# Attention gate's projection as three rounded passes, its rests made by GpSimd

## The reference, cut to what matters

```python
for l in range(DEPTH):                      # 2 layers
    h = rmsnorm_2(x, norm_g[l])             # (256, 1024)
    proj = h @ w_in[l]                      # all projections of the layer
    q, k, v, ga, iq, ik, iw, xr, gr, ma, mb = jnp.split(proj, offsets, axis=-1)
    ...
    attn = dsa_attention(q, k, v, iq, ik, iw).reshape(B, S, ATTN_WIDTH_2)   # 8 heads x 128
    y_a = (attn * jax.nn.silu(ga)) @ w_out_attn[l]
    ...
    hr = rg_lru(xr, w_rg[l], b_rg[l], w_ig[l], b_ig[l], lru_lambda[l])      # a scan over tokens
    y_b = (hr * jax.nn.silu(gr)) @ w_out_rnn[l]
    merged = jax.nn.sigmoid(ma) * y_a + jax.nn.sigmoid(mb) * y_b
    x = x + merged @ w_o[l]
```

## Time and profile before

| what | before |
|---|---|
| median of 3 runs | 1917.48 us |
| lowest, highest | 1916.91, 1917.63 us |
| the profiled execution, its own time | 1915.96 us |
| its span, first to last instruction | 1914.2 us |
| PE (TensorE) busy | 1854.3 us, 97% of the span |
| DVE (VectorE) busy | 833.7 us, 44% |
| ACT (ScalarE) busy | 670.1 us, 35% |
| POOL (GpSimd) busy | 268.8 us, 14% |
| mean granted TensorE clock | 0.992 of full speed |

### The profile page before, as it was taken

The page is one execution under the profiler, slowest core; times in us unless marked ns, Lnnn a source line. Parts: engine busy times, 40 slices in busy tenths (PEclk is TensorE's granted clock), DMA queues, the critical chain, the costliest instruction groups (busy, mean ns, idle before and its releaser), DMA issues.

```text
span 1914.2 us, 28319 instructions
## 1 busy us (share of the span) xinstructions
PE 1854.3 (97%) x11306; PEld 1257.3 (66%) x11306; DVE 833.7 (44%) x1889; ACT 670.1 (35%) x1287; POOL 268.8 (14%) x239
## 2 busy tenths in 40 slices
PE   9999999999999999999999999999999999999998
PEld 8774444444447874444434446888989978888997
DVE  5763121211215762112211114566665655667655
ACT  5632111111114631111111113457664544575544
POOL 1400000000000400000000003972000057800000
PEclk9999999999999999999999999999999999999999
DMA  8569999999996469999999996452524845433353
GB/s 297 225 237 416 428 427 427 429 428 428 429 424 226 189 274 399 412 427 427 428 428 429 429 427 241 143 207 89 173 92 154 280 171 176 174 136 104 118 170 134
DMA packets 121430, 557.58 MB, mean 291 GB/s; under 512 B 5008, under 2 KB 49584, under 8 KB 96240
## 3 DMA queue, kind: packets, MB, share of 16 engines
q1 hardware_dynamic: 119696, 551.51, 72.5%
q10 hardware_dynamic: 1440, 4.36, 0.6%
q0 software_dynamic: 192, 0.30, 0.1%
HBM read 555.11 MB, written 1.05 MB: 291 GB/s over the span
## 4 chain that ended last, share of the span: by engine, by line
PE 58%; DVE 4%; DMA 3%; ACT 3%; issue 2%; POOL 0%; SPq 0%; POOLq 0%; DVEq 0%; ACTq 0%
PE bank L2322 7%; PE bank L2353 5%; PE bank L2471 3%; PE bank L2473 3%; PE bank L2472 3%; DMA ring<-w_up_dram 3%; PE bank L2450 3%; PE bank L2451 3%; PE bank L2452 3%; PE bank L2324 3%; PE bank L2557 3%; PE bank L2045 2%; PE bank L2420 2%; PE bank L2054 2%; PE bank L2487 1%
## 5 line engine op out<-in xcount | busy, mean ns | idle before, releaser
L2322 PE MATMUL bank<-ring,work 128*64 128x512 f32 x544 | 242.6, 601 | 13.4 <-issue 13.4
L1663 DVE TENSOR_TENSOR work<-work,bank 64x512 f32<-64x512 f32 x64 | 43.9, 685 | 440.0 <-ACT work L1004 440.0
L2324 PE MATMUL bank<-ring,work 128*64 128x512 f32 x512 | 232.3, 609 | 0.0
L776 POOL TENSOR_TENSOR stat<-stat,power 128x1 f32<-128x1 f32 (+1 forms) x18 | 10.8, 600 | 1496.5 <-DVE stat L1235 959.9
L816 POOL TENSOR_TENSOR w_lo<-ring,w_hi 128x512 fp32r<-128x512 f32 (+1 forms) x160 | 208.1, 1317 | 53.6 <-ACT w_hi L1054 50.8
L1004 ACT ACTIVATE work<-bank 64x512 f32<-64x512 f32 x64 | 37.8, 591 | 466.5 <-PE bank L2324 466.5
L1054 ACT CAST w_hi<-ring 128x512 fp32r<-128x512 f32 (+1 forms) x208 | 123.3, 606 | 120.8 <-PE bank L2473 81.5
L2353 PE MATMUL bank<-ring,work 128*64 128x512 f32 x480 | 155.8, 595 | 1.8 <-ACT work L1009 0.4
L2322 PEld LDWEIGHTS bank<-ring,work 128*64 128x64 f32 x544 | 73.1, 138 | 125.5 <-issue 123.6
L1883 DVE TENSOR_TENSOR w_lo<-ring,w_hi 128x512 fp32r<-128x512 f32 (+1 forms) x176 | 116.3, 678 | 79.0 <-ACT w_hi L1159 78.7
L1679 DVE SCALAR_TENSOR_TENSOR act_hi<-bank,stat,act_hi 128x512 fp32r<-128x512 f32 x64 | 48.1, 751 | 211.1 <-ACT act_hi L1014 211.1
(11 more groups left out here) (354 smaller groups left out, 4489.4 us busy)
## 6 DMA issues: line engine op xcount, KB each, us to landing
ring<-w_in_dram SPq DMA_DIRECT2D x34, 2048.0 KB, 9.0
ring<-w_gate_dram SPq DMA_DIRECT2D x34, 2048.0 KB, 21.1
ring<-w_up_dram SPq DMA_DIRECT2D x32, 2048.0 KB, 26.6
ring<-w_down_dram SPq DMA_DIRECT2D x30, 2048.0 KB, 26.0
ring_tail<-w_down_dram SPq DMA_DIRECT2D x18, 2048.0 KB, 24.1
work<-w_gate_dram SPq DMA_DIRECT2D x16, 2048.0 KB, 21.8
work<-w_up_dram SPq DMA_DIRECT2D x16, 2048.0 KB, 26.2
ring_tail<-w_up_dram SPq DMA_DIRECT2D x16, 2048.0 KB, 27.2
```

The costliest lines, as they stand in the source:

```text
L2322: pe.matmul(m_bank(m)[gate, :], lhs, wg[:, k], start=(k == 0), stop=(k == KD - 1), skip_group_check=True)
L2324: mu = pe.matmul(m_bank(m)[up, :], lhs, wu[:, k], start=(k == 0), stop=(k == KD - 1), skip_group_check=True)
```

## The change

- `ga` becomes two entries of `SPLIT` (`QGA`), with 16 chunks a layer: each head has two chunks, and a chunk holds four of the eight blocks of 128 input features by 128 output features. `closed_by` says which chunks end with a PSUM tile, since now every second chunk of `ga` does.
- ScalarE rounds each chunk (`round_gate`): the two of head 0 ahead of the last silu gates, the first of head 1 ahead of head 0's exponentials and the second behind them, and from then on the two of head hh + 2 on each side of head hh + 1's exponentials.
- GpSimd makes the 16 rests of a layer, each behind ScalarE's rounding of it.
- TensorE's `gate(hh)` is 24 fp32r products in place of eight float32 ones.
- ScalarE's rounding of `mb`'s first two chunks goes behind the gate of the last head, that of the other two and the three parts of `round_hidden` behind the last transposes. VectorE's rests of them go the same way.

```diff
@@ -578,12 +578,13 @@
                  + [(PXR, ("xr", 3), KD * 512), (PXR + 1, ("xr", 7), KD * 512), (PXR + 2, ("xr", 10), KD * 384)]
                  + [(PV, ("v", 1), KD * 512), (PV + 1, ("v", 3), KD * 512)]
                  + [(PGR, ("gr", 3), KD * 512), (PGR + 1, ("gr", 7), KD * 512), (PGR + 2, ("gr", 10), KD * 384)]
+                 + [(PGA, ("ga", 3), KD * 512), (PGA + 1, ("ga", 7), KD * 512)]
                  + [z for pc in range(4) for z in ((PMB + 2 * pc, None, KD * 256),
                                                    (PMB + 2 * pc + 1, ("mb", 2 * pc + 1), RT * 256))]
                  + [z for pc in range(4) for z in ((PMA + 2 * pc, None, KD * 256),
                                                    (PMA + 2 * pc + 1, ("ma", 2 * pc + 1), KD * 256))]
                  + [(PO, ("out2", 1), KD * 512), (PO + 1, ("out2", 3), KD * 512)])
-        QXR, QV, QGR, QPAIR = 5, 8, 10, 13
+        QXR, QV, QGR, QGA, QPAIR = 5, 8, 10, 13, 15
         PAIRS = 8
         QO = QPAIR + 2 * PAIRS
 
@@ -591,8 +592,18 @@
 
             return KD if SPLIT[q][2] == KD * 384 else -(-SPLIT[q][2] // 512)
 
+        def closed_by(q, c):
+
+            if q in (QGA, QGA + 1):
+                return ("ga", 4 * (q - QGA) + c // 2) if c % 2 else None
+            return SPLIT[q][1] if c == chunks_of(q) - 1 else None
+
+        def marked(q, n):
+
+            return sum(closed_by(q, c) is None for c in range(n))
+
         CHUNK0 = [sum(chunks_of(z) for z in range(q)) for q in range(len(SPLIT) + 1)]
-        MARKED0 = [sum(chunks_of(z) - (SPLIT[z][1] is not None) for z in range(q)) for q in range(len(SPLIT) + 1)]
+        MARKED0 = [sum(marked(z, chunks_of(z)) for z in range(q)) for q in range(len(SPLIT) + 1)]
 
         def chunk(layer, q, c):
 
@@ -602,11 +613,24 @@
 
             layer, r = divmod(g, CHUNK0[-1])
             q = next(z for z in range(len(SPLIT)) if r < CHUNK0[z + 1])
-            c, tile = r - CHUNK0[q], SPLIT[q][1]
-            if tile is not None and c == chunks_of(q) - 1:
+            c = r - CHUNK0[q]
+            tile = closed_by(q, c)
+            if tile is not None:
                 full(eng, (tile[0], layer, tile[1]))
             else:
-                eng.wait_ge(chunk_used, layer * MARKED0[-1] + MARKED0[q] + c + 1)
+                eng.wait_ge(chunk_used, layer * MARKED0[-1] + MARKED0[q] + marked(q, c + 1))
+
+        def gate_chunk(layer, hh, half):
+
+            return chunk(layer, QGA + hh // 4, 2 * (hh % 4) + half)
+
+        def by_k(t, g):
+
+            return t[:, g % CHUNKS].rearrange("p (k n) -> p k n", n=P)
+
+        def gate_words_of(w, hh, half):
+
+            return w[:, KD // 2 * half:KD // 2 * (half + 1), hh % 4 * P:(hh % 4 + 1) * P]
 
         def chunk_words(words, q, c):
 
@@ -814,6 +838,14 @@
                         pool.wait_ge(chunk_hi, g + 1)
                         n = w.shape[2]
                         pool.tensor_tensor(w_lo[:, g % CHUNKS, 0:n], w[:, k], w_hi[:, g % CHUNKS, 0:n], ALU.subtract
+                                           ).then_inc(chunk_lo, 1)
+                for hh in range(HEADS):
+                    w = arrive2(pool, layer, PGA + hh // 4)
+                    for half in range(2):
+                        g = gate_chunk(layer, hh, half)
+                        pool.wait_ge(chunk_hi, g + 1)
+                        pool.wait_ge(chunk_lo, g)
+                        pool.tensor_tensor(by_k(w_lo, g), gate_words_of(w, hh, half), by_k(w_hi, g), ALU.subtract
                                            ).then_inc(chunk_lo, 1)
             inverse_rms(FINAL)
 
@@ -1143,6 +1175,13 @@
                     silu_gates(j)
                 round_weights(QGR + 2, CHUNKS, KD)
 
+                def round_gate(hh, half):
+
+                    w = arrive2(act, layer, PGA + hh // 4)
+                    g = gate_chunk(layer, hh, half)
+                    chunk_left(act, g - CHUNKS)
+                    act.copy(by_k(w_hi, g), gate_words_of(w, hh, half)).then_inc(chunk_hi, 1)
+
                 def exponentials2(hh):
                     act.wait_ge(negmax2, layer * HEADS + hh + 1)
                     st = stat[:, 16 + 8 * (hh % 2):24 + 8 * (hh % 2)]
@@ -1165,23 +1204,33 @@
                                 (act_hi[:, CHUNKS:], ui[:, CHUNKS:KD]))[part]
                     act.copy(dst, src).then_inc(ui_hi_ready, 1)
 
-                act.wait_ge(hidden_ready, layer + 1)
                 def gate(hh):
                     empty(("ga", layer, hh), ga_all[:, hh], bank(("ga", layer, hh))[:, 0:SEQ])
 
+                round_gate(0, 0)
+                round_gate(0, 1)
                 for j in range(8, RT):
                     silu_gates(j)
+                round_gate(1, 0)
                 exponentials2(0)
+                round_gate(1, 1)
+                act.wait_ge(hidden_ready, layer + 1)
                 gate(0)
                 for hh in range(HEADS):
                     empty(("PT2", layer, hh), pT2[:, hh % 2], bank(("PT2", layer, hh))[:, 0:3 * P])
+                    if hh + 2 < HEADS:
+                        round_gate(hh + 2, 0)
                     if hh + 1 < HEADS:
                         exponentials2(hh + 1)
+                        if hh + 2 < HEADS:
+                            round_gate(hh + 2, 1)
                         gate(hh + 1)
-                    if 2 <= hh < 4:
-                        round_words(QPAIR, 2 * (hh - 2), 2 * (hh - 2) + 2)
-                    elif hh >= 5:
-                        round_hidden(hh - 5)
+                    if hh == HEADS - 2:
+                        round_words(QPAIR, 0, 2)
+                round_hidden(0)
+                round_words(QPAIR, 2, 4)
+                round_hidden(1)
+                round_hidden(2)
 
                 def round_merged(k):
 
@@ -1906,11 +1955,13 @@
                     if hh + 1 < HEADS:
                         logits(hh + 1)
                         weights(hh + 1)
-                    if 3 <= hh < 5:
-                        rest_of_words(QPAIR, 2 * (hh - 3), 2 * (hh - 3) + 2)
+                    if hh == HEADS - 1:
+                        dve.wait_ge(chunk_lo, chunk(layer, QPAIR, 0))
+                        rest_of_words(QPAIR, 0, 2)
                     attended(hh)
-                    if hh >= 6:
-                        rest_of_hidden(hh - 6)
+                rest_of_hidden(0)
+                rest_of_words(QPAIR, 2, 4)
+                rest_of_hidden(1)
                 rest_of_hidden(2)
                 rest_of_words(QPAIR + 1)
                 S.settle()
@@ -2572,9 +2623,19 @@
                     emptied(pe, ("v", layer, j))
                 def gate(hh):
                     name = ("ga", layer, hh)
-                    w_ = arrive2(pe, layer, PGA + hh // 4)
                     claim(name)
-                    done(by_feature(bank(name)[:, 0:SEQ], w_, hh % 4), name)
+                    dst = bank(name)[:, 0:SEQ]
+                    for half in range(2):
+                        g = gate_chunk(layer, hh, half)
+                        pe.wait_ge(chunk_lo, g + 1)
+                        for kk in range(KD // 2):
+                            k = KD // 2 * half + kk
+                            pe.matmul(dst, by_k(w_hi, g)[:, kk], hT_hi[:, k], start=(k == 0), stop=False)
+                            pe.matmul(dst, by_k(w_hi, g)[:, kk], hT_lo[:, k], start=False, stop=False)
+                            mm = pe.matmul(dst, by_k(w_lo, g)[:, kk], hT_hi[:, k], start=False, stop=(k == KD - 1))
+                        if half == 0:
+                            mm.then_inc(chunk_used, 1)
+                    done(mm, name)
 
                 scores2(0)
                 gate(0)
```

## The result

Over 20 runs of each kernel the changed one took 1919.86 us and the one before 1916.97 us (medians): ratio 1.0015, 95% interval 1.0009 to 1.0021, that is +2.9 us where +3.3 us was forecast. The profiled execution has a span of 1917.7 us, 3.5 us more.

A forecast was written before the change was run, and what follows sets the result against it. TensorE, busy 97%, bounds the kernel, but a VectorE and ScalarE chain sets heads 0 and 1. Per layer +4.9, -3.4 and +0.2 us give about +1.65 us, two layers +3.3 us: 1920.8 us, range 1914.0 to 1925.5 us.

The forecast's parts named there:

- two rests beside six scans: Head 0's two GpSimd rests fall beside VectorE's last six scans and delay them: +2.2 us a layer.
- rounding ahead of the table: ScalarE rounds head 1's first chunk between silu gates and table load, on the chain: +0.5 us a layer.
- two rests beside eight products: Head 1's second rest and head 2's first fall beside VectorE's eight `gated_hidden` products: +2.2 us a layer.
- six gates: Gates of heads 2 to 7, where TensorE leads, are 0.57 us shorter each: -3.4 us a layer.
- end of the stage: Later roundings and rests around the last product with v and the products behind it: +0.2 us a layer.
- TensorE's part: A gate takes 2.88 us in fp32r instead of 3.45 us; only heads 2 to 7 count, 3.4 us a layer.
- Rounding on ScalarE: Chunk roundings cost nothing, except head 1's first, ahead of the table load: +0.5 us.
- What the rests do to VectorE: Each GpSimd rest beside VectorE work with two SBUF operands adds 1.1 us; four such meetings on each layer's chain.
- Margins: From head 2 on, scales precede transposes by 1.1 us with the faster gate, enough for roundings and rests.
- Rival 3: TensorE's clock falls after longer idle time before the transposes, costing 1.5 us a layer behind the second: 1923.8 us, chance 0.24.
- Rivals 1 and 2: 1: GpSimd and VectorE never meet on chain, 1912.1 us, chance 0.09; 2: only eight products pay, 1916.4 us, chance 0.19.
- rival 4: GpSimd's rests take longer than half a head, from 2.26 us each, and bound the kernel: 1942 us, chance 0.05.

The follow-up runs named there:

- e6: The changed kernel with head 1's first rounding moved behind head 0's exponentials; ratio 1.0022 to the kernel before.
- e1: The kernel before, with two extra unused GpSimd subtractions per layer that read SBUF, beside the last six scans; ratio 1.0025 to the kernel before.
- e2: The kernel before, with four extra GpSimd memsets per layer that only write SBUF, beside the last six scans; ratio 1.0000 to the kernel before.
- e3: The changed kernel with GpSimd's first rest of head 0 held until VectorE's last scan is done; ratio 1.0030 to the kernel before.
- e10: The changed kernel with 14 unused float32 products ahead of TensorE's wait for the first transposes; ratio 1.0041 to the kernel before.
- e8: e7 with ten unused float32 products ahead of TensorE's wait for the first transposes; ratio 0.9981 to the kernel before.
- e7: The changed kernel with the gates of heads 0 and 1 in float32 again and GpSimd's rests not held; ratio 0.9993 to the kernel before.
- e9: The changed kernel with head 1's second rest held until the eight gated products are done, plus 14 unused TensorE products; ratio 1.0022 to the kernel before.

## Why the prediction was right

**The number** was 1920.8 us against a median of 1917.5 us, +3.3 us; measured were +2.9 us. Its terms, for one layer, as measured in the first:

| term | forecast | measured | from |
|---|---|---|---|
| two rests beside six scans | +2.2 | +2.1 | 5.73 - 3.60 |
| rounding ahead of the table | +0.5 | +0.64 | e6 |
| two rests beside eight products | +2.2 | +2.2 | 4.97 - 2.77 |
| six gates | -3.4 | -3.5 | 5.0 + 0.1 - 1.6 |
| end of the stage | +0.2 | +0.1 | idle 0.91 against 0.82 |
| sum | +1.65 | +1.6 | stage |

**TensorE's part** held: 2.87 us a gate, forecast 2.88. The second transposes were 5.0 us later in the stage and the last product 1.6 us later, so 3.5 us were won from there, with 0.1 us lost at the end.

**Rounding on ScalarE** held, with a part that the forecast left out: the negation of head 0's maxima waited for the rest of head 1 (1.19 us in place of 0.17) and held the exponentials up by some 0.15 us. That is within the 0.64 us; the rounding itself is the other 0.5 us.

**What the rests do to VectorE.** The bounds for a scan were 0 and 1.1 us a rest and I took the upper one from lines 1731 and 1733; e1 shows it alone. e2 narrows the mechanism: a GpSimd instruction that reads SBUF counts, one that only writes it doesn't. Each of GpSimd's instructions, 1.3 to 1.5 us long, costs a row of VectorE's instructions with two operands in SBUF 1.0 to 1.1 us; the three products without a rest keep their 1.10 us. The Trainium skill ("SBUF — State Buffer", "Who interferes with whom") has a VectorE instruction with two inputs in SBUF contend with a GpSimd instruction that reads SBUF, and not with one that only writes; these runs agree. VectorE's `tensor_scalar` with one operand was held up too (the negation above, and the first scale of head 2, 0.62 us in place of 0.29; TensorE did not notice that one). No experiment took these two apart from the rest, so that GpSimd is the cause there is not shown.

**Margins** of the later heads held: their first transposes are 4.5 us apart, as TensorE alone sets.

**Rival 3, the clock, was there and was free.** The windows of PE in the changed kernel, first layer:

```profile
1376.00:1380.00 4.00, 0.28 (x4) 1.00 0.17 52
1380.00:1384.00 4.00, 4.00 (x25) 0.60 0.00 0
1384.00:1388.00 4.00, 2.19 (x15) 0.97 0.00 0
```

It fell behind the first idle stretch (4.17 us), and the slower gate was paid out of the second, which shrank from the forecast 3.3 us to 1.81 us, in the second layer to 0.68 us. So it went as the rival's own counter-argument had it: the first fall spends the second idle stretch, and the clock did not fall where TensorE leads. This is read from one execution of the changed kernel. The price that the rival named, 1.5 us a layer behind the second stretch, is what e3 paid (6.0 against 4.5 us); e10 paid 2.7 us in one layer. Rivals 1 and 2 are ruled out by the scans and products, rival 4 by rests of 1.3 to 1.5 us.

## What to carry to other kernels

Work taken off the busiest engine counts only where that engine leads; find the stretches where it waits, and leave those alone: with two of eight heads left in float32, and GpSimd's rests kept off VectorE's scans and products, a loss of 3 us became a gain of 7 us. Work given to GpSimd is not free because GpSimd is idle: look for VectorE instructions with two operands in SBUF on the chain beside it, and place GpSimd's reads where none stand. Filling TensorE's idle time to keep its clock paid where the next thing was TensorE's own (e8, 2 us); where another engine set the time it moved the fall to a worse place (e10).

## What was not expected

- The clock's fall can shield: the slow gate of head 1 kept TensorE from sitting idle, and e10, which took the fall away from that gate, was slower (1.0041, 1.0027 to 1.0055, against 1.0015, 1.0009 to 1.0021).
- A held GpSimd instruction does not slip past a short row of VectorE work: in e3 three products of 1.1 us held both rests, because the first made the row long enough for the second. The same hold also gave TensorE's waits another order, which cost more than the hold could win.
- The length of an idle stretch alone does not tell whether the clock falls. Stretches of 2.9 us (e7, both layers) and of 4.2 us (changed kernel) were followed by the lower clock, the 0.8 us of the kernel before were not. In between, the same stretch was followed by it in one layer and not in the other of the same execution: 2.77 us in e1, 2.06 and 2.07 us in e9, 3.4 us in e10. What decides there stays open.
